# Hybrid streaming-encoder layer on one core: in branch A the products with the values, two blocks back, are placed in front of the turns of the last block's probabilities

## The reference, cut to what matters

```python
def block(i):                       # 128 queries, keys 0 .. (i+1)*128
    s = einsum('bqhmd,bkhmd->bhmqk', qb, k) * scale + bias[None, :, None]
    s = where(mask, s, NEG_INF)
    p = softmax(s, axis=-1)         # two maps, m = 0 and 1
    attn = p[:, :, 0] - lam * p[:, :, 1]
    return einsum('bhqk,bkhe->bqhe', attn, vf)
```

## Time and profile before

| | |
|---|---|
| median of 3 runs | 1786.45 us |
| the profiled execution | 1786.02 us, its span 1784.2 us |
| granted clock, mean over the span | 0.999 |
| TensorE matmul busy | 1759.4 us, 99% of the span |
| VectorE, ScalarE, GpSimd busy | 60%, 42%, 37% |
| branch A | about 56 to 497 us of the span |

### The profile page before, as it was taken

One profiled execution on the slowest core, in us unless ns is written; L12 is line 12 of the kernel. 1 busy time (PEld: TensorE's weight loads), 2 busy tenths in 40 slices (PEclk: granted clock), 3 DMA queues, 4 the chain that ended last, 5 costly groups with the idle time before them and its releaser, 6 DMA issues.

```text
span 1784.2 us, 25435 instructions
## 1 busy us (share of the span) xinstructions
PE 1759.4 (99%) x8815; PEld 1476.5 (83%) x8815; DVE 1076.9 (60%) x2359; ACT 741.7 (42%) x1592; POOL 659.0 (37%) x659
## 2 busy tenths in 40 slices
PE   6999999999999999999999999999999999999998
PEld 4888888888888888888888888888888888888886
DVE  6577777777665552013424654866666677777667
ACT  5566666666566665201321232322333332222232
POOL 4311112112134442222222340655566566555570
PEclk9999999999999999999999999999999999999999
DMA  5611111111211101134333430221111111111212
GB/s 180 209 37 49 33 49 43 43 38 45 47 39 34 33 25 36 48 118 142 95 95 118 131 106 1 83 63 56 47 47 47 47 47 57 60 47 47 71 35 95
DMA packets 143543, 117.91 MB, mean 66 GB/s; under 512 B 23572, under 2 KB 130268, under 8 KB 143452
## 3 DMA queue, kind: packets, MB, share of 16 engines
q1 hardware_dynamic: 134236, 112.52, 20.5%
q10 hardware_dynamic: 9216, 4.20, 0.8%
HBM read 99.88 MB, written 21.53 MB: 68 GB/s over the span
## 4 chain that ended last, share of the span: by engine, by line
PE 96%; DVE 2%; ACT 1%; DMA 0%; issue 0%; POOL 0%; SPq 0%; DVEq 0%; ACTq 0%
PE bank L596 28%; PE bank L598 28%; PE bank L597 27%; PE bank L622 4%; PE bank L701 4%; PE bank L684 2%; PE bank L633 1%; PE bank L685 1%; PE bank L650 0%; DMA res<-in_x_dram 0%; DVE small L1427 0%; POOL y_lo L1319 0%; ACT mix L1085 0%; DVE y_lo L1705 0%; DVE mix L1446 0%
## 5 line engine op out<-in xcount | busy, mean ns | idle before, releaser
L596 PE MATMUL bank<-hT_hi,w_hi 128*128 128x512 f32 x1296 | 513.9, 397 | 0.6 <-POOL hT_lo L1273 0.4
L598 PE MATMUL bank<-hT_hi,w_lo 128*128 128x512 f32 x1296 | 506.1, 391 | 0.0
L597 PE MATMUL bank<-hT_lo,w_hi 128*128 128x512 f32 x1296 | 505.4, 390 | 0.0
L1250 POOL TENSOR_TENSOR w_lo<-w_raw,w_hi 128x256 fp32r<-128x256 f32 x260 | 184.9, 742 | 584.5 <-ACT w_hi L902 584.5
L596 PEld LDWEIGHTS bank<-hT_hi,w_hi 128*128 128x128 f32 x1296 | 243.6, 188 | 52.4 <-POOL hT_lo L1273 1.3
L598 PEld LDWEIGHTS bank<-hT_hi,w_lo 128*128 128x128 f32 x1296 | 243.6, 188 | 52.3
L597 PEld LDWEIGHTS bank<-hT_lo,w_hi 128*128 128x128 f32 x1296 | 243.9, 188 | 47.5
L596 PE MATMUL bank<-y_hi 128*128 128x512 f32 (+1 forms) x548 | 205.9, 376 | 0.0
L597 PE MATMUL bank<-y_lo,y_hi 128*128 128x512 f32 (+1 forms) x548 | 203.3, 371 | 0.0
L598 PE MATMUL bank<-y_hi,y_lo 128*128 128x512 f32 (+1 forms) x548 | 203.2, 371 | 0.0
L1339 POOL TENSOR_TENSOR y_lo<-y_full,y_hi 128x512 fp32r<-128x512 f32 x98 | 132.7, 1376 | 166.8 <-ACT y_hi L1185 166.8
(11 more groups left out here) (205 smaller groups left out, 2977.8 us busy)
## 6 DMA issues: line engine op xcount, KB each, us to landing
w_raw<-in_w_in_dram SPq DMA_DIRECT2D x100, 256.0 KB, 3.3
w_raw<-in_w_ff_dram SPq DMA_DIRECT2D x64, 256.0 KB, 4.0
y_full<-in_w_ff_dram SPq DMA_DIRECT2D x32, 512.0 KB, 3.7
bias_rows<-bias_line SPq DMA_DIRECT2D x3, 1536.0 KB
res<-in_x_dram SPq DMA_DIRECT2D x8, 512.0 KB, 7.0
x_spill<-res SPq DMA_DIRECT2D x8, 512.0 KB, 5.0
o_spill<-o_buf ACTq DMA_DIRECT2D x64, 64.0 KB, 1.6
w_raw<-in_w_branch_b_dram SPq DMA_DIRECT2D x16, 256.0 KB, 3.8
```

Of the source, the lines that this page charges most:

```text
L596: pe.matmul(bank, lhs[0], rhs[0], start=start, stop=False)
L597: pe.matmul(bank, lhs[0], rhs[1], start=False, stop=False)
L598: return pe.matmul(bank, lhs[1], rhs[0], start=False, stop=stop)
L1250: ins = pool.tensor_tensor(w_tile(n, 1)[:, at:at + 2], w_raw[:, at:at + 2, :], w_tile(n, 0)[:, at:at + 2].bitcast(F32), ALU.subtract)
```

## The change

In each step of branch A from step 2 on, `attend_a` of the step two back is called ahead of the turns of the step before, no longer behind them. Nothing else is touched: in block 1 the turns of the values stand where they stood, now directly behind the turn of block 0. The other engines' programs are the same. The passage to branch B is the same.

```diff
                             if i >= 4:
                                 block_a(1)
+                            if step >= 2:
+                                attend_a((step - 2) // NT, (step - 2) % NT)
                             if step >= 1:
                                 for b in range(1 + (step - 1) % NT // 4):
                                     pe.wait_ge(probs_ready, probs_count(step - 1) + b + 1)
                                     transposes(("pa", (step - 1) // NT, (step - 1) % NT, b))
-                            if step >= 2:
-                                attend_a((step - 2) // NT, (step - 2) % NT)
                             if i == 1:
                                 pe.wait_ge(freed_act, freed(True, LAST[TILE[("va", h)]]))
                                 for b in range(2):
```

## The result

| | before | after |
|---|---|---|
| median of 17 runs each | 1786.46 us | 1789.86 us |
| ratio, 95% interval | | 1.0019 (1.0013 to 1.0025) |
| profiled execution | 1786.02 us, span 1784.2 | 1791.65 us, span 1789.9 |
| span of a second profile, same kernel | | 1787.9 us (1789.74 in all) |

The change costs 3.4 us; 4.9 were forecast. So it is read together with a second one.

The account below looks back on a forecast made before the run. TensorE's own queue was taken as the bound (busy 1759.4 of 1784.2 us). Terms 3.35 + 0.35 + 0.3 - 0.46 + 0.2 + 1.2 = 4.9 us on 1786.02, with 0.43 for the median, gave 1791.4; range 1788.9 to 1794.2.

Parts of the forecast that it names:

- the line of 1790.0: Whole run: boundary between same and slower, about 0.2% or 3.6 us; chances 0.76 slower, 0.22 same, 0.02 faster.
- the first rival's milder form: Whole run: (a) holds, the passage to branch B hides (g), (b) and (c) come to 0.4; 1789.8 us, chance 0.14.
- (g): End of branch A: products before block 6's turns delay the bound chain into branch B; +1.2 us, bounds 0 and 1.4.
- (c): Seams between matmul kinds in the other 55 steps: changes nearly cancel; +0.3 us, bounds -1.6 and +1.6.
- (a): Block 1, heads 1 to 7: the values' third batch waits for its bank; 0.48 us each, +3.35, lower bound 0.
- (b): Seam in block 1: the nearly free single transpose costs a run's 0.11 us; 0.05 each, +0.35 in all.
- (d): Turns in block 0, heads 1 to 5: waits for line 1543 go; -0.46 us, bounds -0.46 and 0.
- (e): Block 7's products wait for VectorE's sum (line 1530): 0.03 us for each of 7 heads, +0.2, bounds 0 and 1.
- its signs of being wrong: Trace after: eight bank waits absent, or TensorE waiting for line 1530 or scores by tenths in many blocks.
- (f): Elsewhere in a head: delays of ScalarE, VectorE, GpSimd and SyncE stay hidden; cost 0.
- the first (no bank wait): Block 1: both engines empty a single transpose's bank in time, so (a) does not appear; 1788.0 us, chance 0.08.
- The second, lateness through ScalarE's exponentials: Block 1: late exponentials delay ScalarE's copy, adding 0.3 to 0.6 us a head to the round trip; 1794.4, chance 0.13.

Follow-up runs that it names:

- Block 1 alone in front: Against the kernel before, products ahead of the turns in block 1 only, behind them in all other blocks: 1790.06 us, ratio 1.0020.
- sum first: The full change, plus VectorE's sum (line 1530) ahead of the cuts of the turns in block 0 of each head: 1788.83 us, ratio 1.0012 to the kernel before.
- block 1 behind: Against the kernel before, products ahead of the turns in all blocks but block 1: 1786.71 us, ratio 1.0002.
- last step in front: Against the kernel before, products ahead of the turns only in the last block of the last head: 1788.22 us, ratio 1.0008.
- scores between: The full change, plus the scores of block 2 between the values' two batches of turns in block 1: 1786.00 us, ratio 0.9998 to the kernel before.

## Why the prediction was right, and where its terms were off

The measured median lies in the range, 1.5 under the forecast. The main mechanism forecast, the bank's round trip in block 1, is the one found, and so is the delay at the entry to branch B. That the total is this near is in part luck, as errors of the other terms went against each other. At 1789.86 the time stands on the line of 1790.0 itself, on its near side, so that 0.76 on the far side was too much. It is also the 1789.8 of the first rival's milder form, but not by its mechanism: the entry hid nothing of (g), and it was (c) that came out lower.

(a) Right: 3.35 forecast, 3.34 measured. In the second profile the third batch starts 0.53 behind the transpose ahead of it and its second transpose 0.165 behind its first, where 0.109 is ordinary: 0.48 a head. That price was read from a case that the kernel before already held, head 0, and it carried the forecast.

(b) and (c), the seams, are where the sum failed. I took +0.35 and +0.3. Block 1 alone in front measured (a) and (b) together at 3.34, so (b) is about 0: the transpose costs 0.11 in place of 0.03, and the pair behind the group gives 0.09 back. Measured for (c): -1.35 in blocks 2 to 7, and in block 0 -0.96 less the 0.46 of waits, -0.50, so -1.85 us, outside its bound of -1.6. The failed step is "after: no extra in the pair": I set the first pair of products behind a 512-column matmul at the ordinary 0.17. In the kernel after, block 2 of head 7 reads:

```profile
460.12 0.39 PE L598 MATMUL bank<-hT_hi,w_lo 128*128 128x512 f32 x1
460.12 0.19 PEld L684 LDWEIGHTS bank<-y_hi,y_lo 128*128 128x128 f32 x1
460.35 0.28 PE L684 MATMUL bank<-y_hi,y_lo 128*128 128x256 f32 x1
460.35 0.19 PEld L685 LDWEIGHTS bank<-y_hi,y_lo 128*128 128x128 f32 x1
460.46 0.22 PE L685 MATMUL bank<-y_hi,y_lo 128*128 128x128 f32 x1
460.52 0.41 PE L622 MATMUL bank<-ident,mix 128*128 128x128 f32 x2
460.68 0.48 PE L596 MATMUL bank<-hT_hi,w_hi 128*128 128x512 f32 x1
461.00 0.39 PE L597 MATMUL bank<-hT_lo,w_hi 128*128 128x512 f32 x1
```

460.35 to 460.46 is 0.11: behind a long matmul a pair is 0.06 cheaper than in a run and 0.09 cheaper than behind transposes. The loads of weights show why. In the kernel before, behind the transpose at 451.15:

```profile
451.15 0.19 PEld L684 LDWEIGHTS bank<-y_hi,p_more 128*128 128x128 f32 x1
...
451.26 0.19 PEld L685 LDWEIGHTS bank<-y_hi,p_more 128*128 128x128 f32 x1
```

Each of the 273 matmuls of line 685 between 60 and 500 us starts 0.11 to 0.13 after its own load starts, in the profile before, the one after and that of the sum first. Behind a transpose the first product's load starts 0.03 ahead of it (451.15, 451.18), so the partner's load comes 0.08 after the first product (451.26), and the partner at 451.38. Behind a 512-column matmul the first product's load starts 0.23 ahead (460.12), the partner's load starts together with the first product (460.35), and the partner follows 0.11 later.

Added up over the 54 steps of (c), second profile against the one before, first pairs gave 4.2 us. The starts of groups took 1.2 back (0.32 here against 0.28, as forecast); two seams that I had left out took more: the first two transposes behind products, 0.126 apart in place of 0.109, 0.8, and scores behind transposes 0.5. The net is 0.03 a step in the mean, but not evenly: 0.07 in block 0 and 0.09 in block 2, 0.01 to 0.02 in the others. In blocks 0 and 2 the matmuls inside the half groups also run a little closer than before (0.227 in place of 0.231 in head 7), in blocks 3 to 7 a little wider; why, no run shows. The rule of the Trainium skill ("TensorE: Matmul & The Clock Gate", "What happens when you issue a matmul" and "LDWEIGHTS") that the next weights load under the running matmul agrees with these loads. By its figure for a load, an estimate of 107 ns for 128 columns, (b) and (c) would be 0: that is right for (b), and 1.85 us off for (c).

(d) Right against this profile of the kernel before, -0.46; that the old waits vary between executions (0.9 and 1.2 in the two other profiles with the old order in block 0) was not known.

(e) Too small: 0.2 forecast, 4.69 - 3.37 = 1.32 measured, beyond its bound of 1. The chain and its length were right: the sum ends 3.62 us after the turns of block 0 start (449.77 to 453.39), 3.61 forecast. Two steps failed. I gave the semaphore 0.06 after the sum's end, and the products start 0.14 after it; and I did not price what a held start costs behind it, the 0.08 of the pair. With 0.19 us of it in seven blocks, a wait for line 1530 that the forecast had among its signs of being wrong was there, in small.

(f) Right: no new wait in blocks 2 to 7.

(g) Right: 1.2 forecast, 1.18 to 1.20 measured in the three profiles with the longer wait and without the half clock. What was missing is the half clock itself.

The three largest errors are -2.15 for (c), +1.1 for (e) and -0.35 for (b), which together bring the forecast's 4.9 down to 3.5. Of the rivals, the first (no bank wait) fell with the eight waits. The second, lateness through ScalarE's exponentials, did not lengthen the round trip: the copy at 455.73 still found ScalarE idle for 0.33. It did show in block 1's old order, with 0.14 a head (0.94 against 0.80), and there through the same bank.

## What to carry to other kernels

When work is moved out from between two uses of a buffer, ask what the buffer's round trip was hidden behind, and look for a place where the kernel already runs without that cover: its rows give the price. In a full queue an order is worth what its seams are worth, some 0.03 to 0.1 us each, so read a seam from a row of the same pair of neighbours, and its loads of weights with it, not from the ordinary row. A moved block should take with it, on the other engines, the step that it frees or feeds; here the sum ahead of the cuts and the scores between the batches turned +3.4 us into -3.2, together with the old order kept in the last step, where the delay had no cover.

## What the runs showed of the hardware that was not expected

The changed kernel and four of the others (block 1 behind, last step in front, sum first, scores between) have a TensorE wait of 1.6 us at the entry to branch B. Counted by the mean clock of 0.998 or less that runs with the stretch show, it came in 15 of their 72 runs (1 of 17 and 2 of 11 for the changed kernel, 3, 3, 2 and 4 of 11 for the others, in that order), each 0.7 to 1.8 us above the median of its kernel. The three profiles that have it fall to half the clock (1.2 in place of 2.4 GHz) 0.9 to 1.8 us after the wait's end, with TensorE busy all that time. Of 99 runs of kernels whose wait there is 0.43 us (66 of the kernel before), one had a low mean clock. So a wait longer by 1.2 us can cost its own length again, in about one execution in five. Which executions it strikes stays open: the three profiles with the stretch came to branch A 0.40 to 0.45 us later than the kernel before's, the three with the same wait and without the stretch 0.08 to 0.19 earlier, which may be chance.

A unit held by a semaphore starts later than its release by different amounts: 0.06 us after a cut's end, 0.14 after the sum's. And a pair of short matmuls behind it is 0.08 slower (0.19 against 0.11): in the trace the load of the held product's weights is held with it (453.50, where an unheld one starts 0.23 ahead of its product), and the partner's load comes behind it. Why the loads stand 0.11 apart no run takes apart.
